# Weight-block sums of a seven-product scheme moved from VectorE to GpSimd (fp32 encoder trunk, one core)

## The reference

```python
h = rms_norm(x, norm_w[layer])
z = h @ w_in                      # 4096 x (13312 or 10240)
y = attention(z) * silu(gate(z))  # heads of 128
x = x + y @ w_out                 # 4096 x 4096
```

## Time and profile before

| | |
|---|---|
| median of 3 runs | 2795.7 us (2795.07 to 2796.16) |
| the profiled execution's own time | 2795.44 us |
| its span in the trace | 2793.7 us |
| PE busy | 2778.2 us, 99% |
| VectorE busy | 1891.2 us, 68% |
| ScalarE busy | 1402.5 us, 50% |
| GpSimd busy | 16.4 us, 1% |
| granted TensorE clock | 0.999 of full speed |

### The profile page before, as it was taken

How to read it: one execution, slowest core, us unless ns; L and a number is a source line. 1 busy time by engine, 2 the same in 40 slices (tenths; PEclk the granted TensorE clock), 3 DMA queues, 4 the chain that set the end, 5 groups by cost and what they waited for, 6 DMA issues and landing times.

```text
span 2793.7 us, 36061 instructions
## 1 busy us (share of the span) xinstructions
PE 2778.2 (99%) x12591; PEld 2311.7 (83%) x12591; DVE 1891.2 (68%) x2338; ACT 1402.5 (50%) x1717; POOL 16.4 (1%) x14
## 2 busy tenths in 40 slices
PE   9999999999999999999999999999999999999998
PEld 7888888888888888887888888888888888888886
DVE  7766756576666765469787676666667666668785
ACT  6455555455454544445454455555545555544443
POOL 0000000000000000000000000000000000000000
PEclk9999999999999999999999999999999999999999
DMA  9777777777777777677777767777766777676766
GB/s 334 220 213 231 227 222 224 221 226 230 230 214 222 225 221 240 191 253 247 249 257 224 227 213 225 233 231 219 222 213 219 240 227 222 221 250 209 225 205 203
DMA packets 357930, 637.26 MB, mean 228 GB/s; under 512 B 25376, under 2 KB 79136, under 8 KB 357792
## 3 DMA queue, kind: packets, MB, share of 16 engines
q1 hardware_dynamic: 343824, 593.52, 68.3%
q10 hardware_dynamic: 13968, 41.95, 4.2%
HBM read 585.56 MB, written 49.81 MB: 227 GB/s over the span
## 4 chain that ended last, share of the span: by engine, by line
PE 94%; DVE 4%; DMA 1%; issue 0%; ACT 0%; DVEq 0%; POOLq 0%; POOL 0%; SPq 0%; ACTq 0%
PE proj L1439 30%; PE proj L1440 30%; PE proj L1441 30%; DVE w_lo L988 1%; PE o_bank L1440 1%; PE o_bank L1439 1%; PE sc_ps L1441 1%; PE o_bank L1441 1%; PE sc_ps L1440 1%; PE sc_ps L1439 1%; DMA raw<-in_w_out_c 1%; PE m L1439 0%; PE m L1440 0%; PE m L1441 0%; DVE w_lo L998 0%
## 5 line engine op out<-in xcount | busy, mean ns | idle before, releaser
L988 DVE TENSOR_TENSOR w_lo<-raw,w_hi 128x1024 fp32r<-128x1024 f32 x930 | 1134.2, 1220 | 619.7 <-ACT w_hi L801 611.7
L801 ACT ACTIVATE w_hi<-raw 128x1024 fp32r<-128x1024 f32 x930 | 985.5, 1060 | 898.5 <-PE proj L1441 777.4
L1439 PE MATMUL proj<-w_hi,h_hi 128*128 128x512 f32 x2852 | 1110.3, 389 | 1.0 <-DVE w_lo L988 1.0
L1440 PE MATMUL proj<-w_lo,h_hi 128*128 128x512 f32 x2852 | 1110.2, 389 | 0.0
L1441 PE MATMUL proj<-w_hi,h_lo 128*128 128x512 f32 x2852 | 1109.4, 389 | 0.0
L1441 PEld LDWEIGHTS proj<-w_hi,h_lo 128*128 128x128 f32 x2852 | 535.3, 188 | 111.5
L1439 PEld LDWEIGHTS proj<-w_hi,h_hi 128*128 128x128 f32 x2852 | 535.5, 188 | 109.2 <-DVE w_lo L988 1.4
L1440 PEld LDWEIGHTS proj<-w_lo,h_hi 128*128 128x128 f32 x2852 | 535.5, 188 | 106.9
L1439 PE MATMUL proj<-w_hi,y_hi 128*128 128x512 f32 x928 | 361.2, 389 | 0.6 <-DVE w_lo L988 0.6
L1440 PE MATMUL proj<-w_lo,y_hi 128*128 128x512 f32 x928 | 361.1, 389 | 0.0
L1441 PE MATMUL proj<-w_hi,y_lo 128*128 128x512 f32 x928 | 361.0, 389 | 0.0
(11 more groups left out here) (291 smaller groups left out, 1606.4 us busy)
## 6 DMA issues: line engine op xcount, KB each, us to landing
raw<-in_w_in_ab SPq DMA_DIRECT2D x414, 512.0 KB, 4.4
raw<-in_w_in_c SPq DMA_DIRECT2D x320, 512.0 KB, 4.4
raw<-in_w_out_ab SPq DMA_DIRECT2D x128, 512.0 KB, 4.5
raw<-in_w_out_c SPq DMA_DIRECT2D x128, 512.0 KB, 4.5
head_turn<-head_stage SPq DMA_DIRECT2D x256, 96.0 KB, 1.9
head_land<-head_turn ACTq DMA_DIRECT2D x64, 384.0 KB, 5.5
landing<-group_turn ACTq DMA_DIRECT2D x31, 512.0 KB, 5.0
group_turn<-q_stage SPq DMA_DIRECT2D x64, 128.0 KB, 3.3
```

The lines of the kernel that those rows point to most:

```text
L801: nc.scalar.activation(w_hi[:, slot], raw[:, m % RING], ACT.Copy).then_inc(hi_ready, 1)
L988: nc.vector.tensor_tensor(w_lo[:, slot], raw[:, m % RING], w_hi[:, slot].bitcast(F32), ALU.subtract) \
L1439: nc.tensor.matmul(dst, hi, r_hi, start=start, stop=False, skip_group_check=more)
L1440: nc.tensor.matmul(dst, hi, r_lo, start=False, stop=False, skip_group_check=more)
```

## The change

The four subtractions of each quad are issued by GpSimd (`weight_sums`, a new function in its block) and no longer by `quad_lo` of VectorE. GpSimd now walks the same pairs as the other engines, so that its nine powers stand among the sums in program order. It waits for the same semaphores as VectorE did: for the loads of b12, b22 and b21, for lo(0), lo(2) and lo(4), and for its own sum before. Waits that VectorE had only for the sums are gone from it. ScalarE, TensorE and SyncE run the same instructions as before.

```diff
--- before.py
+++ after.py
@@ -747,11 +747,54 @@
             nc.gpsimd.memset(minus_half[:], -0.5).then_inc(minus_half_set, 1)
             pool.wait_ge(minus_half_set, 1)
 
-            for n, (dst, cols) in enumerate([(rms, slice(0, TT))] + [(head_rms, slice(0, TT * HB))] * 5
-                                            + [(rms, slice(0, TT)), (rms, slice(0, 1)), (rms, slice(1, 2))]):
+            def power(n, dst, cols):
+
                 pool.wait_ge(var_ready, n + 1)
                 nc.gpsimd.tensor_tensor(dst[:, cols], var[:, cols], minus_half[:, cols], ALU.pow) \
                     .then_inc(pow_done, 1)
+
+            def weight_sums(p, k, start):
+
+                n, done = p.o + p.op[start], QUAD * (p.quad_n + k)
+                mix, mix3 = (tile[:] for tile in mix_of[p.out])
+                slots = [(start + r) % RING for r in range(QUAD)]
+                b11, b12, b22, b21 = (raw[:, slot] for slot in slots)
+                minus = lambda dst, a, b: nc.gpsimd.tensor_tensor(dst, a, b, ALU.subtract).then_inc(mixed, 1)
+
+                def landed(r):
+
+                    pool.wait_ge(raw_loaded[slots[r]], 16 * (p.n * (NB // RING) + (start + r) // RING + (slots[r] > 1)))
+
+                pool.wait_ge(lo_ready, n + 1)
+                landed(1)
+                minus(mix, b12, b11)
+                landed(2)
+                pool.wait_ge(mixed, done + 1)
+                minus(mix3, b22, b12)
+                pool.wait_ge(lo_ready, n + 3)
+                pool.wait_ge(mixed, done + 2)
+                minus(mix, b22, mix)
+                landed(3)
+                pool.wait_ge(lo_ready, n + 5)
+                pool.wait_ge(mixed, done + 3)
+                minus(b21, b21, mix)
+
+            def body(p):
+                if p.n0 == 0:
+                    power(0, rms, slice(0, TT))
+                if p.side == "k_norm":
+                    power(1, head_rms, slice(0, TT * HB))
+                    power(2, head_rms, slice(0, TT * HB))
+                if p.side == "A" and p.out == "qg":
+                    power(p.batch + 3, head_rms, slice(0, TT * HB))
+                if p.n0 == X1_FIRST + 4:
+                    power(6, rms, slice(0, TT))
+                for k, start in enumerate(p.quads):
+                    weight_sums(p, k, start)
+
+            walk(pool, body)
+            for t in range(TT):
+                power(7 + t, rms, slice(t, t + 1))
 
         @block.scalar
         def _(act):
@@ -993,8 +1036,7 @@
 
                 n = p.o + p.op[start]
                 mix, mix3 = (tile[:] for tile in mix_of[p.out])
-                mixes_done = QUAD * (p.quad_n + k)
-                b11, b12, b22, b21 = (raw[:, (start + r) % RING] for r in range(QUAD))
+                b11, _, b22, b21 = (raw[:, (start + r) % RING] for r in range(QUAD))
                 minus = lambda dst, a, b: nc.vector.tensor_tensor(dst, a, b, ALU.subtract)
 
                 def lo(r, source, count=1):
@@ -1006,26 +1048,13 @@
                 if part == 0:
                     lo(0, b11)
                 if part == 1:
-                    second = (start + 1) % RING
-                    dve.wait_ge(raw_loaded[second], 16 * (p.n * (NB // RING) + (start + 1) // RING + (second > 1)))
-                    dve.wait_ge(lo_ready, n + 1)
-                    minus(mix, b12, b11).then_inc(mixed, 1)
                     lo(1, b22)
                 if part == 2:
-                    dve.wait_ge(mixed, mixes_done + 1)
-                    minus(mix3, b22, b12).then_inc(mixed, 1)
                     lo(2, mix)
-                    dve.wait_ge(mixed, mixes_done + 2)
-                    dve.wait_ge(lo_ready, n + 3)
-                    minus(mix, b22, mix).then_inc(mixed, 1)
                     lo(3, mix3)
                 if part == 3:
                     lo(4, b21)
-                    dve.wait_ge(mixed, mixes_done + 3)
-                    dve.wait_ge(lo_ready, n + 5)
-                    minus(b21, b21, mix).then_inc(mixed, 1)
                     lo(5, mix)
-                    dve.wait_ge(mixed, mixes_done + 4)
                     lo(6, b21, 2)
                     dve.wait_ge(lo_ready, n + OPS)
 
```

## The result

The changed kernel takes **2886.7 us** (median of 4 runs, 2881.5 to 2888.3) against 2795.4 us before: ratio 1.0323, 95% interval 1.0310 to 1.0336. The forecast was 2862 with a range of 2803 to 2890: the direction and the exclusion of the two engines were right, and the time came out 25 us short, mostly because the clock was costed at nothing. The profiled execution took 2881.5 us, the fastest of the four; its span is 2879.7 us, 86.0 more than before.

The account below looks back on a forecast made before the run. TensorE was taken to bound the kernel, with VectorE's lead scarce in the quads. Fifteen quads at 5.5 us, 82.5, less slack 9.3, less 6.0 for b22 waits, gave 67 us: 2795.4 + 67 = 2862 us, range 2803 to 2890.

Parts of the forecast that it names:

- exclusion: VectorE instructions with two SBUF inputs and GpSimd instructions reading SBUF take turns; with a sum near 2.4 us, chance 0.58.
- the clock: Rival: TensorE's waits halve its clock, 1 to 3 us a quad, 2890 us; chance 0.07, shared with dearer GpSimd under exclusion.
- the slack at the end of a quad: VectorE's lead left before product 6, between 0 and 1.4 us a quad, 9.3 us over fifteen quads, subtracted from the loss.
- VectorE's relief: Sixty subtractions of 1.22 us leave VectorE, 4.9 us a quad; alone this can return only TensorE's 3.3 us of waits.
- Price of a sum: One subtraction on GpSimd: 2.45 us, twice VectorE's 1.22, with 1.22 and 3.7 as ends.
- The chain of a quad: From lo(0) to lo(6), splits and sums in turn: lo(6) ends 5.5 us later a quad, 82.5 us over fifteen.
- the dearer schedule: First come, first served in the first quad, lo(3) and lo(5) ahead of the third and fourth sums: lo(6) 6.3 us later.
- The waits for b22: Where VectorE waited for ScalarE's copy of b22, the first sum runs in that wait, giving back 6.0 us.
- Loads and powers at nothing: SyncE's next-block loads, moved by 1 to 5 us, and GpSimd's powers were expected to cost nothing.
- Dear GpSimd without exclusion: Rival: a sum costs 3.7 us and engines run freely; lo(6) 5.4 us later, 2861 us, splits stay 1.22 us; chance 0.07.
- partial exclusion: Rival: splits slip between GpSimd's reads or only splits stretch; lo(5) and lo(6) some 2.5 us late, 2817 us; chance 0.14.
- hidden sums: Rival: engines run freely and sums follow only their data; 2800 us, or 2792 with sums of 1.22 us; chance 0.14.

Follow-up runs that it names:

- idle subtractions: Kernel before, plus four GpSimd subtractions of two SBUF tiles, results unused, beside each of the last four quads: 2826.2 us, ratio 1.0111.
- memsets: Kernel before, plus eight GpSimd memsets of a free tile, reading nothing, beside each of the last four quads: 2795.7 us, ratio 0.9998.
- filled waits: Changed kernel, plus zero-tile matmuls in each quad, 4 ahead of product 4 and 13 ahead of product 6: 2864.3 us, ratio 1.0249.
- sums first: Changed kernel, but VectorE waits for the third sum before lo(3) and for the fourth before lo(5): 2867.0 us, ratio 1.0254.
- fourth sum alone: Changed kernel, but only the fourth sum (b21 - mix) stays on GpSimd, the others back on VectorE: 2816.8 us, ratio 1.0070.

## Why the prediction was right, and where it fell short

- **What bounds the kernel.** Right: the slack at the end of a quad decided. The 3.3 us that VectorE's relief could return never showed.
- **Price of a sum.** Taken as 2.45 us, measured 2.40 where the way is free, as in the first sum of the first quad. The Trainium skill's ratio of 1.96 (GPSIMD Engine Reference, Elementwise — side-by-side cycle accounting), stated for 2048 columns, gives with VectorE's 1.22 us an estimate of 2.4. This trace agrees: 2.40 against 1.22 us is 1.97.
- **Exclusion.** Right, in both directions now: shown by the records after, and shown to be no matter of data by the idle subtractions. The rule of the Trainium skill (SBUF — State Buffer, Who interferes with whom) is borne out in its parts. Two SBUF inputs meet a reading GpSimd and are held (3.4 us instead of 1.22). They are not held against one that only writes (1.22 us beside the memsets). Nor is a VectorE instruction with one SBUF input (0.69 us, the additions from PSUM).
- **The chain of a quad.** Taken 5.5 us later, from schedules of 5.3 and 6.3; measured 17.47 − 12.17 = 5.3. The order is that of the dearer schedule, lo(3) and lo(5) ahead of the third and fourth sum; each of its ten steps was about 0.1 us shorter than I had it (held instructions take 2.24 and 1.09 us from end to end, not 2.45 and 1.22). The schedule that gave 5.3 hit the number by another order.
- **The waits for b22.** Taken as giving back 6.0 us; the fifteen distances from lo(0) to lo(6) grew by 73.5 us, against 15 x 5.3 = 79.5, so 6.0.
- **The sum.** With these, 79.5 − 6.0 − 9.3 = 64 us, where I had 67. The starts of the same matmuls, compared between the traces before and after, agree: summed over the fifteen quads, product 6 starts 63.0 us later. The other 23.1 of the 86.0 us come behind that start, 10.8 inside product 6 and 12.3 in the blocks right behind the quads. The kernel with filled waits stands at 69 over the kernel before (2864.3 − 2795.5; 68.2 in the profiled executions). There product 6 starts 65.9 us later and only 2.3 come behind it. Of the 2.9 by which 65.9 is more than 63.0, 2.3 lie in three quads: in the fifth and the fourteenth lo(0) ends 1.0 and 0.7 us less ahead of product 0, and in the eighth lo(6) ends later. Whether the fillers do that is not shown.
- **The step that failed** was to cost the clock at nothing in the likeliest case. As the prediction put it, the clock was a rival of 1 to 3 us a quad, 2890, with a chance of 0.07 that it shared with a dearer GpSimd. It came on top of the exclusion, not in its place: 22.4 us by the filled kernel and 23.1 by the trace, some 2 us in each of the eleven quads where the clock fell. The reason given for a low chance, that no row has such a gap inside the work, was no evidence against it: the prediction itself put up to 4 us of waiting in one piece there. The likeliest case should have been 2862 + 22 = 2884. The measured time lies in the stated range only because that rival set its upper end.
- **Loads and powers at nothing.** Right for the loads: with the clock kept up, 1.1 us was lost outside the quads in the whole kernel. For the powers nothing in the runs speaks against it.
- **The rivals.** Dear GpSimd without exclusion, partial exclusion and hidden sums all fell by the records: every split and every sum that met the other ends a fixed time behind it (1.08 to 1.09 us, 2.24 to 2.26 us), so the two never share.

## What to carry to other kernels

In these runs, moving elementwise work with two SBUF inputs from VectorE to GpSimd bought no parallel time where VectorE's own work had two SBUF inputs: add the durations of both queues, at GpSimd's price, as if they were one engine. VectorE's additions out of PSUM ran beside GpSimd's subtractions, and GpSimd's memsets ran beside VectorE's subtractions. When a forecast contains waits of TensorE of 2 to 3 us in one piece, price matmuls at half clock too. Here the clock fell in eleven of fifteen quads with waits of 3 us, in eleven places with waits of 1.8 to 2.1 us (sums first), and in two of the eight quads with a late lo(6) (fourth sum alone). A filler in the wait shows the share in one run.

## What the hardware showed that I had not expected

A larger count of matmuls made the kernel faster: 255 matmuls with a zero tile, 22.4 us less, by keeping the granted clock at 1.00. The order of two short splits against two sums, by two waits more, was worth 19.7 us, of which only 9.1 remain when the clock is kept up. In the changed kernel a held split or sum always ended the same time behind the other engine's instruction, to 0.02 us. And one GpSimd subtraction a quad costs 5 us as the first of the chain and 21 as its last, some 3.5 of them the clock's.
